# A fourth K pair by seven products in the strips of both up projections

## The chip, the cores and the metric

The kernel runs on one core of one Trainium2 chip. The metric is the device time of one execution in microseconds. The kernel before takes 2373.14 us, the median of 3 runs (2372.95 to 2373.27).

## The reference, cut to what matters

```python
D_MODEL, SEQ, FFN_HIDDEN = 2048, 256, 5632

def swiglu(x, w_up, w_down):
    g, u = jnp.split(x @ w_up, 2, axis=-1)
    return (jax.nn.silu(g) * u) @ w_down

h = h + 0.5 * rms_norm(swiglu(rms_norm(h, ffn1_pre), ffn1_up, ffn1_down), ffn1_post)
h = h + rms_norm(hybrid_mixer(rms_norm(h, mix_pre), ...), mix_post)
h = h + 0.5 * rms_norm(swiglu(rms_norm(h, ffn2_pre), ffn2_up, ffn2_down), ffn2_post)
```

All is float32 with 256 tokens. `x @ w_up` is 256 x 2048 by 2048 x 11264; its left half is the gate, its right half the upper part. Each of the two feed-forward blocks has such an up projection, and the change is in these two.

## The kernel before

A float32 product is made of three fp32r matmuls: high part by high part, low part by high part, high part by low part (the helper `three`, and the same in `products`). So each weight block that TensorE (PE) takes must first be split: SyncE loads 256 rows x 512 columns (a "group", 128 partitions x 1024 elements, 512 KB) into one of four slots of `w_raw`; ScalarE (ACT) rounds it to `w_hi` (`round_group`, L1260); VectorE (DVE) subtracts to get `w_lo` (`rest_group`, L1641). Both work four groups ahead of TensorE: at loop position n they treat group n+4, and the rounding waits until TensorE has used group n in the same slot. SyncE loads into a slot of `w_raw` again as soon as DVE has made `w_lo` of it, and, where sums are made of it, once these are made too (`up_loads`).

An up projection is cut into 11 strips of 512 gate columns and the 512 upper columns that go with them. The first strip is a stage of its own (`first0`, `first1`), computed plainly. The other ten (`NST`) are a loop, the stages `up0` and `up1`. A strip has 16 groups, of which eight are for the gate and eight for the upper part; K (2048) is eight K groups ("pairs", since each has two tiles of 128 rows). Plain, a pair takes one gate group and one upper group, each 2 row tiles x 2 token tiles x 3 matmuls, so 24 matmuls of 512 columns for both.

Three pairs (`QUADS`) are computed otherwise, with seven block products in place of eight, in the manner of Strassen and Winograd: over the 2 x 2 blocks (two row tiles; gate and upper) sums of weight blocks are multiplied by sums of token blocks, 21 matmuls in all. The token sums `s_hi`, `s_lo` are made once, in the stage `first`. The weight sums are made anew for each pair in each strip:

- `sum13` (DVE, L1829) makes two of four sums at once, 1024 elements, and needs both groups of the pair landed; it stands ahead of the `rest_group` of the pair's gate group;
- `sum24` (DVE, L1837 and L1839) makes the third and the fourth, 512 elements each, behind that `rest_group`;
- ACT rounds the four sums in two instructions of 1024 elements (L1458), at the positions in `T_AT`, and DVE subtracts in two instructions of 1024 elements (L2024), behind the `rest_group` of the same positions. For a pair whose gate group is ng these positions are ng-3 and ng-2;
- of the pair's upper group only half need be split (`w_cols`), 512 elements in place of 1024.

Two buffers hold the sums (`T_SLOT`), and `sum13` waits on `t_used` for the one it writes. TensorE computes a pair at the position of its upper group (`seven_products`, L870 to L872), in this order: two products with split weights of the gate group, one of the upper group, then two products for which it waits for the first of the two splits of sums (`t_split`), one for which it waits for the second, and one more. Four PSUM banks collect products of all pairs of a strip; DVE combines them in four instructions at n = 13, two at n = 14, and four, with two block transposes, after the last group (L2030 to L2055, L1978).

In the last strip DVE and ACT also split the first two parts of the hidden activations (`hidden_hi`, `hidden_lo`, L1680) at n = 12 to 14, which the first matmul of the stage `down` needs. All engines take their instructions in order; the order is written out by hand.

Of the kernel before, what the change touches and what calls it, by code (L numbers as in the profile page):

```python
# [23 lines left out]
P = 128  # L24
D = 2048
SEQ = 256
MT = SEQ // P
# [23 lines left out]
WARM_UP = 2  # L51


QUADS = ((5, 6, 5), (9, 10, 6), (12, 13, 7))
PLAIN_GATE = ((0, 0), (1, 1), (2, 2), (3, 3), (4, 4))
PLAIN_UP = ((7, 0), (8, 1), (11, 2), (14, 3), (15, 4))
NQUAD = len(QUADS)
NST = NUP - 1
S_TILES = 2 * NQUAD
# [92 lines left out]
def hybrid_trunk(nc, t, out):  # L152
    f32, f32r = mybir.dt.float32, mybir.dt.float32r
# [16 lines left out]
    with ctx:  # L170
# [3 lines left out]
        def sb(name, shape, dt, at=None):  # L174
            size = 4
            for n in shape[1:]:
                size *= n
            if at is None:
                at = place["at"]
                place["at"] += -(-size // 32) * 32  # L180
            return nc.alloc_sbuf_tensor_at(name, shape, dt, offset=at)

        h = sb("h", [P, MT, D], f32)
        x_at = place["at"]
# [43 lines left out]
        r_end = r_hi + 4 * KF * SEQ  # L228
# [10 lines left out]
        s_x = r_hi + 32 * 2 * STRIP  # L239
        s_raw = sb("s_raw", [P, 4, NQUAD, P], f32, at=s_x)  # L240
        s_lo = sb("s_lo", [P, 4, NQUAD, P], f32r, at=s_x)
        s_hi = sb("s_hi", [P, 4, NQUAD, P], f32r, at=s_x + 16 * NQUAD * P)
        assert s_x + 32 * NQUAD * P <= r_end
        h_scaled = sb("h_scaled", [P, S_TILES * P], f32, at=r_hi)
        a_tile0 = sb("a_tile0", [P, S_TILES, P], f32, at=r_hi + 4 * S_TILES * P)
        a_tile1 = sb("a_tile1", [P, S_TILES, P], f32, at=r_hi + 8 * S_TILES * P)
# [118 lines left out]
        t_used = sem("t_used")  # L365
# [7 lines left out]
        h_parked = sem("h_parked")  # L373
# [106 lines left out]
        def quad(f, i, j):  # L480

            return (NQUAD * NST + NDQ) * f + NQUAD * i + j
# [8 lines left out]

        QUAD_GATE = {ng: j for j, (ng, nu, k) in enumerate(QUADS)}
        QUAD_UP = {nu: j for j, (ng, nu, k) in enumerate(QUADS)}
        DQ_A = [{ng: j for j, (ng, nu, k) in enumerate(quads)} for quads in DOWN_QUADS]
        DQ_B = [{nu: j for j, (ng, nu, k) in enumerate(quads)} for quads in DOWN_QUADS]
        T_SLOT = (1, 0, 1)

        COMBINED = ("u4", "hid")

        def wait_combined(eng, f, i, what):  # L500

            eng.wait_ge(combined, len(COMBINED) * (NST * f + i) + COMBINED.index(what) + 1)

        def w_cols(sec, i, n):

# [3 lines left out]
        def t_pair(a, j, pair):  # L509

            return a[:, T_SLOT[j], 2 * pair:2 * pair + 2, :]

        T_AT = {ng - 3 + pair: (j, pair) for j, (ng, nu, k) in enumerate(QUADS) for pair in range(2)}

# [10 lines left out]
        def wait_quad_used(eng, f, i, j):  # L525

            eng.wait_ge(t_used, quad(f, i, j) + 3)
# [16 lines left out]
        SQUARES, at = {}, 0  # L544
# [23 lines left out]
        def _(sp):  # L568
# [14 lines left out]
            def up_loads(f):  # L583
                for n in range(2 * GD):
                    load(f"first{f}", 0, n, up[f][n % GD][:, :, (n // GD) * FFN:(n // GD) * FFN + STRIP])
                    if f == 0 and n in (0, 1, 3, 4):
# [3 lines left out]
                        else:  # L590
                            load_x((n + 2) // 2)
                source = {n: (k, 0) for n, k in PLAIN_GATE}
                source.update({n: (k, FFN) for n, k in PLAIN_UP})
                for ng, nu, k in QUADS:
                    source[ng], source[nu] = (k, 0), (k, FFN)
# [167 lines left out]
        def _(pe):  # L763
# [110 lines left out]
            def scaled_transposes(f):  # L874

                pe.wait_ge(h_scaled_ready, f + 1)
                for b, tiles in ((2, range(0, 2)), (3, range(2, S_TILES))):
                    claim(f"s{f}", b)
                    for x in tiles:
                        last = transpose(bank[b][:, x % 4 * P:(x % 4 + 1) * P], h_scaled[:, x * P:(x + 1) * P])  # L880
                    last.then_inc(filled[b], 1)

            def seven_products(f, i, j):

                sec = f"up{f}"
                ng, nu, k = QUADS[j]
                first, last = j == 0, j == NQUAD - 1
# [12 lines left out]
                def tt(y):  # L900
                    return t_hi[:, T_SLOT[j], y, :], t_lo[:, T_SLOT[j], y, :]

# [69 lines left out]
            def swiglu(f):  # L972
# [15 lines left out]
                with pe.Fori(0, NST) as i:  # L988
                    sec = f"up{f}"
                    gate_of, up_of = dict(PLAIN_GATE), dict(PLAIN_UP)  # L990
                    for n in range(2 * GD):
# [256 lines left out]
        def _(act):  # L1248
# [179 lines left out]
            def swiglu(f):  # L1428
                sec = f"first{f}"
                for n in range(2 * GD):  # L1430
                    round_group(sec, 0, n)
                    if f == 0 and n in (0, 2):
                        x_hi(n // 2 + 2)
                    if n == (3 if f == 0 else 2):
                        if f == 0:
                            for c in range(CH):
                                act.wait_ge(x_landed[c], 16)
                        input_squares(2 * f)
                    if n == GD - 1:
                        wait_strip(act, sec, 0, n)  # L1440
                        act.wait_ge(rs_ready, MEAN[f"pre{2 * f}"] + 1)
                        pair = pair_of(sec, 0)
                        for m in range(MT):
                            last = act.activation(gate_sb[:, m, :], acc[pair][m][:, :], ACT.Silu,
                                                  scale=rs_pre[:, 2 * f, m:m + 1])
                        last.then_inc(acc_read[pair], 1)
                    if n == 14:
                        act.wait_ge(s_summed, f + 1)
                        act.activation(s_hi[:, :, :, :].rearrange("p a b n -> p (a b n)"),
                                       s_raw[:, :, :, :].rearrange("p a b n -> p (a b n)"), ACT.Copy).then_inc(s_rounded, 1)  # L1450
                sec = f"up{f}"
                with act.Fori(0, NST) as i:
                    for n in range(2 * GD):
                        round_group(sec, i, n)
                        if n in T_AT:
                            j, pair = T_AT[n]
                            act.wait_ge(t_summed, 3 * quad(f, i, j) + 2 * pair + 1)
                            act.activation(t_pair(t_hi, j, pair), t_pair(t_raw, j, pair), ACT.Copy).then_inc(t_rounded, 1)  # L1458
                        if n == 12:
                            wait_filled(act, f"p{f}", 0, i)  # L1460
                            act.activation(p1_sb[:, :], bank[0][:, :], ACT.Copy).then_inc(read[0], 1)
                        if n == 15:
                            wait_strip_read(act, sec, i, 0)
                            for m in range(MT):
                                last = act.activation(gate_sb[:, m, :], gate_sb[:, m, :], ACT.Silu,
                                                      scale=rs_pre[:, 2 * f, m:m + 1])
                            last.then_inc(silu_done, 1)
                        if n in (12, 13):
                            with act.If(i > NST - 2):
                                if n == 12:  # L1470
                                    wait_quad_used(act, f, NST - 1, 1)
                                hidden_hi(f, n - 12)
                if f == 0:
                    act.wait_ge(consts_landed, 16 * NCONST)
                wait_quad_used(act, f, NST - 1, NQUAD - 1)
                for i in range(CH // 2):
                    down_strips(f, i)
# [150 lines left out]
        def _(dve):  # L1628
# [162 lines left out]
            def scaled_turned(f):  # L1791

                gain = pre_gain[:, 2 * f, :]
                for b, tiles in ((2, range(0, 2)), (3, range(2, S_TILES))):
                    wait_filled(dve, f"s{f}", b)
                    for x in tiles:
                        last = dve.tensor_scalar(a_tile1[:, x, :], bank[b][:, x % 4 * P:(x % 4 + 1) * P],
                                                 gain[:, S_K0 + x:S_K0 + x + 1], None, ALU.mult)
                    if b == 2:
                        last.then_inc(read[b], 1)  # L1800
                last.then_inc(read[3], 1)
# [20 lines left out]
            def sum13(f, i, j):  # L1822

                sec, (ng, nu, k) = f"up{f}", QUADS[j]
                b = quad_blocks(j)
                dve.wait_ge(t_used, quad(f, i, j) + (2 if j == 0 else 1))
                dve.wait_ge(w_landed[ng % SLOTS], group_landed(sec, i, ng))
                dve.wait_ge(w_landed[nu % SLOTS], group_landed(sec, i, nu))
                dve.tensor_tensor(t_pair(t_raw, j, 0), b[:, 0::3, :], b[:, 2:3, :].broadcast_to([P, 2, STRIP]),  # L1829
                                  ALU.add).then_inc(t_summed, 1)  # L1830

            def sum24(f, i, j):

                b = quad_blocks(j)
                t = t_raw[:, T_SLOT[j], :, :]
                dve.wait_ge(t_summed, 3 * quad(f, i, j) + 1)
# [484 lines left out]
```

## Time and profile before

| | |
|---|---|
| median of 3 runs | 2373.14 us |
| the profiled execution | 2372.41 us, its span 2370.6 us |
| TensorE busy, share of the span | 2356.8 us, 99% |
| VectorE busy | 1750.5 us, 74% |
| ScalarE busy | 1243.2 us, 52% |
| GpSimd busy | 205.9 us, 9% |
| DMA | 477.44 MB, mean 201 GB/s |
| TensorE clock granted, mean | 0.999 of full speed |

Busy time is the union of an engine's instructions. The profile's duration of a matmul, 389 ns, is from its start to its modelled end, and matmuls overlap: what counts is the distance from start to start. On DVE too an instruction starts somewhat before the end of the one ahead is shown, so costs on it are also read from start to start. The lines of the trace give the start in us, the duration in us, engine, line of the kernel, operation and tiles; in square brackets stands how long the engine had been idle and what released it.

### The profile page before, as it was taken

To read this page: it belongs to the slowest core of one execution; us is meant where nothing else is said; L and a number is where in the kernel's file an instruction comes from. 1 tells how busy PE (TensorE), PEld (TensorE's weight loads), DVE (VectorE), ACT (ScalarE), POOL (GpSimd) and SP (SyncE) were. 2 spreads that over 40 slices of the span, in tenths; PEclk is the share of its full clock that TensorE was granted. 3 is DMA by queue.
4 is the path that set the end of the run, shared out by engine and by line. 5 is a ranking of instruction groups with operands and counts; after the bars stand their busy time and mean duration, and the time that the engine had idled before them with its cause. 6 is when DMAs were issued, how large, how long until landed. Compare 5 with 4: busy or idle time off the path is not lost. (4 is left out here: it accounts for less than half of the span.)

```text
span 2370.6 us, 33710 instructions
## 1 busy us (share of the span) xinstructions
PE 2356.8 (99%) x10613; PEld 1945.0 (82%) x10613; DVE 1750.5 (74%) x2057; ACT 1243.2 (52%) x1490; POOL 205.9 (9%) x398
## 2 busy tenths in 40 slices
PE   9999999999999999999999999999999999999998
PEld 7888888888888888888888888888888888888887
DVE  6999999978876555655545545555799999997886
ACT  6555555555545454444544444444655555555553
POOL 1212112110000000000000000000021211211000
PEclk9999999999999999999999999999999999999999
DMA  7766666665675555565656566655666666666665
GB/s 236 220 212 203 216 219 222 212 221 191 209 240 172 163 175 178 159 188 157 204 187 196 190 198 193 189 185 194 207 213 227 206 218 207 221 212 214 204 204 195
DMA packets 266605, 477.44 MB, mean 201 GB/s; under 512 B 21152, under 2 KB 54608, under 8 KB 265392
## 3 DMA queue, kind: packets, MB, share of 16 engines
q1 hardware_dynamic: 252752, 453.04, 59.6%
q0 software_dynamic: 13616, 23.53, 3.0%
q8 instruction: 35, 0.57, 0.1%
q14 instruction: 26, 0.21, 0.0%
q10 hardware_dynamic: 176, 0.07, 0.0%
HBM read 460.84 MB, written 4.19 MB: 196 GB/s over the span
## 5 line engine op out<-in xcount | busy, mean ns | idle before, releaser
L1260 ACT ACTIVATE w_hi<-w_raw 128x1024 fp32r<-128x1024 f32 (+1 forms) x848 | 863.6, 1021 | 985.9 <-PE acc L781 732.1
L1641 DVE TENSOR_TENSOR w_lo<-w_raw,w_hi 128x1024 fp32r<-128x1024 f32 (+1 forms) x848 | 991.8, 1172 | 507.5 <-ACT w_hi L1260 503.0
L779 PE MATMUL acc<-w_hi,xT_hi 128*128 128x512 f32 x1552 | 609.2, 393 | 1.0 <-DVE w_lo L1641 1.0
L781 PE MATMUL acc<-w_hi,xT_lo 128*128 128x512 f32 x1552 | 604.4, 389 | 0.0
L780 PE MATMUL acc<-w_lo,xT_hi 128*128 128x512 f32 x1552 | 604.1, 389 | 0.0
L779 PEld LDWEIGHTS acc<-w_hi,xT_hi 128*128 128x128 f32 x1552 | 291.4, 188 | 63.0 <-issue 2.5
L781 PEld LDWEIGHTS acc<-w_hi,xT_lo 128*128 128x128 f32 x1552 | 291.3, 188 | 61.1
L780 PEld LDWEIGHTS acc<-w_lo,xT_hi 128*128 128x128 f32 x1552 | 291.5, 188 | 59.3
L696 POOL DMA_DIRECT2D act_raw<-blocks x352 | 174.9, 497 | 736.4 <-DVE blocks L1978 647.5
L779 PE MATMUL acc<-w_hi,act_hi 128*128 128x512 f32 x560 | 218.2, 390 | 0.1
L780 PE MATMUL acc<-w_lo,act_hi 128*128 128x512 f32 x560 | 217.9, 389 | 0.0
L781 PE MATMUL acc<-w_hi,act_lo 128*128 128x512 f32 x560 | 217.9, 389 | 0.0
L870 PE MATMUL acc<-w_hi,xT_hi 128*128 128x512 f32 x460 | 178.9, 389 | 0.0
L871 PE MATMUL acc<-w_lo,xT_hi 128*128 128x512 f32 x460 | 178.9, 389 | 0.0
L872 PE MATMUL acc<-w_hi,xT_lo 128*128 128x512 f32 x460 | 178.9, 389 | 0.0
L2024 DVE TENSOR_TENSOR t_lo<-t_raw,t_hi 128x1024 fp32r<-128x1024 f32 x120 | 146.2, 1218 | 0.0
L1458 ACT ACTIVATE t_hi<-t_raw 128x1024 fp32r<-128x1024 f32 x120 | 126.8, 1057 | 31.1 <-DVE t_raw L1829 22.1
L779 PEld LDWEIGHTS acc<-w_hi,act_hi 128*128 128x128 f32 x560 | 105.2, 188 | 22.6 <-DVE act_lo L1680 0.9
L781 PEld LDWEIGHTS acc<-w_hi,act_lo 128*128 128x128 f32 x560 | 105.1, 188 | 21.8
L780 PEld LDWEIGHTS acc<-w_lo,act_hi 128*128 128x128 f32 x560 | 105.1, 188 | 21.8
L871 PEld LDWEIGHTS acc<-w_lo,xT_hi 128*128 128x128 f32 x460 | 86.3, 188 | 18.0
L870 PEld LDWEIGHTS acc<-w_hi,xT_hi 128*128 128x128 f32 x460 | 86.3, 188 | 17.9
(269 smaller groups left out, 2601.4 us busy)
## 6 DMA issues: line engine op xcount, KB each, us to landing
w_raw<-in_ffn_up_dram SPq DMA_DIRECT2D x352, 512.0 KB, 4.2
w_raw<-in_ffn_down_dram SPq DMA_DIRECT2D x176, 512.0 KB, 4.2
w_raw<-in_w_gate_dram SPq DMA_DIRECT2D x96, 512.0 KB, 3.8
w_raw<-in_w_in_dram SPq DMA_DIRECT2D x72, 512.0 KB, 3.6
w_raw<-in_w_in_dram SPq DMA_DIRECT2D x128, 256.0 KB, 2.9
w_raw<-in_w_ret_out_dram SPq DMA_DIRECT2D x32, 512.0 KB, 3.7
w_raw<-in_w_out_dram SPq DMA_DIRECT2D x32, 512.0 KB, 4.2
act_raw<-blocks POOLq DMA_DIRECT2D x352, 32.0 KB, 3.8
```

Source lines behind the costliest of these rows:

```text
L696: pool.dma_start(act_raw[to * SQ:(to + 1) * SQ, ds(p, 1), q, :, :, :].rearrange("p a m k i -> p (a m) k i"), blocks[q * SQ:(q + 1) * SQ, t ...
L779: pe.matmul(pair[m][:, :], xh, wh, start=(first and kk == 0), stop=False)
L780: pe.matmul(pair[m][:, :], xh, wl, start=False, stop=False)
L781: mm = pe.matmul(pair[m][:, :], xl, wh, start=False, stop=(last and kk == KG - 1))
L870: pe.matmul(dst, xh, wh, start=start, stop=False)
L871: pe.matmul(dst, xh, wl, start=False, stop=False)
L872: return pe.matmul(dst, xl, wh, start=False, stop=stop)
L1260: act.activation(w_hi[:, s, cols], w_raw[:, s, cols], ACT.Copy).then_inc(w_rounded, 1)
L1458: act.activation(t_pair(t_hi, j, pair), t_pair(t_raw, j, pair), ACT.Copy).then_inc(t_rounded, 1)
L1641: dve.tensor_tensor(w_lo[:, s, cols], w_raw[:, s, cols], w_hi[:, s, cols].bitcast(f32), ALU.subtract).then_inc(w_split, 1)
L2024: dve.tensor_tensor(t_pair(t_lo, j, pair), t_pair(t_raw, j, pair), t_pair(t_hi, j, pair).bitcast(f32), ALU.subtract).then_inc(t_split, 1)
```

## The change

QUADS gets a fourth member. K pair 4 (gate group 4, upper group 5) is added, and pair 5 moves from groups 5 and 6 to groups 6 and 7; pairs 6 and 7 stay at 9, 10 and 12, 13. Four gate groups and four upper groups stay plain. The pairs take the two buffers of sums in turn. The arrays of token sums grow from six tiles to eight (`S_TILES`), so two more transposes and longer DVE and ACT instructions in `first0` and `first1`. The array `s_hi` moves to the place of the residual h; for the second block the instruction that writes it waits until h has been stored to memory (`h_parked`).

```diff
-QUADS = ((5, 6, 5), (9, 10, 6), (12, 13, 7))
-PLAIN_GATE = ((0, 0), (1, 1), (2, 2), (3, 3), (4, 4))
-PLAIN_UP = ((7, 0), (8, 1), (11, 2), (14, 3), (15, 4))
+QUADS = ((4, 5, 4), (6, 7, 5), (9, 10, 6), (12, 13, 7))
+PLAIN_GATE = ((0, 0), (1, 1), (2, 2), (3, 3))
+PLAIN_UP = ((8, 0), (11, 1), (14, 2), (15, 3))
...
-        s_hi = sb("s_hi", [P, 4, NQUAD, P], f32r, at=s_x + 16 * NQUAD * P)
-        assert s_x + 32 * NQUAD * P <= r_end
+        s_hi = sb("s_hi", [P, 4, NQUAD, P], f32r, at=x_at - 4 * MT * D)
+        assert s_x + 16 * NQUAD * P <= r_end
...
-        T_SLOT = (1, 0, 1)
+        T_SLOT = (0, 1, 0, 1)
...
+        PARKED = 16 * MT * 1
...
-                for b, tiles in ((2, range(0, 2)), (3, range(2, S_TILES))):
+                for b, tiles in ((2, range(0, 4)), (3, range(4, S_TILES))):
...
                     if n == 14:
                         act.wait_ge(s_summed, f + 1)
+                        if f == 1:
+                            act.wait_ge(h_parked, PARKED)
                         act.activation(s_hi[:, :, :, :].rearrange("p a b n -> p (a b n)"),
...
                                 if n == 12:
-                                    wait_quad_used(act, f, NST - 1, 1)
+                                    wait_quad_used(act, f, NST - 1, 2)
...
-                dve.wait_ge(t_used, quad(f, i, j) + (2 if j == 0 else 1))
+                dve.wait_ge(t_used, quad(f, i, j) + 1)
```

The line with the tiles changes the same way on DVE (`scaled_turned`).

## Rows read from the trace of the kernel before

**Rows 1.** The page: shares of the span, DVE in slices, ACT's rounding of weights.

```profile
PE 2356.8 (99%) x10613; PEld 1945.0 (82%) x10613; DVE 1750.5 (74%) x2057; ACT 1243.2 (52%) x1490; POOL 205.9 (9%) x398
...
DVE  6999999978876555655545545555799999997886
...
L1260 ACT ACTIVATE w_hi<-w_raw 128x1024 fp32r<-128x1024 f32 (+1 forms) x848 | 863.6, 1021 | 985.9 <-PE acc L781 732.1
```

**Rows 2.** Windows: the stages up0 and up1; header row names the columns.

```profile
core 0: us, PE busy (x) PEld busy (x) DVE busy (x) ACT busy (x) POOL busy (x), PEclk, DMA share, GB/s
57.40:472.20 414.80, 414.80 (x1831) 343.24 (x1829) 388.07 (x429) 234.27 (x253) 79.47 (x160) 1.00 0.67 215
...
1713.70:2128.50 414.80, 414.80 (x1831) 343.28 (x1829) 387.99 (x430) 234.32 (x253) 79.52 (x160) 1.00 0.67 215
```

**Rows 3.** Timeline of TensorE: transposes; first up0 matmul; last; first of down0.

```profile
11.57 1.03 PE L800 MATMUL bank<-ident,h 128*128 128x128 f32 x8
...
57.35 0.39 PE L779 MATMUL acc<-w_hi,xT_hi 128*128 128x512 f32 x1
...
471.93 0.39 PE L872 MATMUL acc<-w_hi,xT_lo 128*128 128x512 f32 x1
472.39 0.50 PE L779 MATMUL acc<-w_hi,act_hi 128*128 128x512 f32 x1
```

**Rows 4.** Timeline of DVE: end of one strip and most of the next.

```profile
142.75 0.68 DVE L2048 TENSOR_TENSOR hid_sb<-acc,u_sb 128x512 f32<-128x512 f32 x1
...
146.87 1.18 DVE L1641 TENSOR_TENSOR w_lo<-w_raw,w_hi 128x1024 fp32r<-128x1024 f32 x1
147.97 1.21 DVE L1829 TENSOR_TENSOR t_raw<-w_raw 128x1024 f32<-128x1024 f32 x1
149.10 1.22 DVE L1641 TENSOR_TENSOR w_lo<-w_raw,w_hi 128x1024 fp32r<-128x1024 f32 x1
150.24 0.68 DVE L1837 TENSOR_TENSOR t_raw<-t_raw,w_raw 128x512 f32<-128x512 f32 x1
150.96 0.69 DVE L1839 TENSOR_TENSOR t_raw<-t_raw,w_raw 128x512 f32<-128x512 f32 x1
151.56 0.68 DVE L1641 TENSOR_TENSOR w_lo<-w_raw,w_hi 128x512 fp32r<-128x512 f32 x1
152.17 1.22 DVE L2024 TENSOR_TENSOR t_lo<-t_raw,t_hi 128x1024 fp32r<-128x1024 f32 x1
...
158.00 1.23 DVE L1829 TENSOR_TENSOR t_raw<-w_raw 128x1024 f32<-128x1024 f32 x1 [1.21 <-DMA w_raw<-in_ffn_up_dram]
...
165.99 1.23 DVE L1829 TENSOR_TENSOR t_raw<-w_raw 128x1024 f32<-128x1024 f32 x1 [0.29 <-DMA w_raw<-in_ffn_up_dram]
...
175.19 1.23 DVE L1641 TENSOR_TENSOR w_lo<-w_raw,w_hi 128x1024 fp32r<-128x1024 f32 x1 [0.36 <-ACT w_hi L1260]
176.62 1.23 DVE L1641 TENSOR_TENSOR w_lo<-w_raw,w_hi 128x1024 fp32r<-128x1024 f32 x1 [0.20 <-ACT w_hi L1260]
177.76 0.68 DVE L2030 TENSOR_TENSOR u_sb<-p_sb,bank 128x512 f32<-128x512 f32 x1
...
180.37 1.23 DVE L1641 TENSOR_TENSOR w_lo<-w_raw,w_hi 128x1024 fp32r<-128x1024 f32 x1
```

**Rows 5.** DMA issues: source, queue, count, KB each, median us to landing.

```profile
w_raw<-in_ffn_up_dram SPq DMA_DIRECT2D x352, 512.0 KB, 4.2
...
out_dram<-h POOLq DMA_DIRECT2D x2, 1024.0 KB, 4.1
```

**Rows 6.** Timeline of DVE: the passage from first0 into up0.

```profile
60.26 1.75 DVE L2000 TENSOR_TENSOR s_lo<-s_raw,s_hi 128x1536 fp32r<-128x1536 f32 x1
...
64.59 1.18 DVE L1641 TENSOR_TENSOR w_lo<-w_raw,w_hi 128x1024 fp32r<-128x1024 f32 x1
```

**Rows 7.** Timeline of DVE: the last strip of up0.

```profile
462.23 1.22 DVE L2024 TENSOR_TENSOR t_lo<-t_raw,t_hi 128x1024 fp32r<-128x1024 f32 x1
...
471.05 1.29 DVE L1680 TENSOR_TENSOR act_lo<-act_raw,act_hi 128x512 fp32r<-128x512 f32 x2
```

**Rows 8.** Timeline of GpSimd: the second store of h.

```profile
1672.48 0.53 POOL L752 DMA_DIRECT2D out_dram<-h  x1 [3.69 <-DVE h L1713]
```

More of the change, by code:

```diff
@@ L1793, in scaled_turned @@
                 gain = pre_gain[:, 2 * f, :]
-                for b, tiles in ((2, range(0, 2)), (3, range(2, S_TILES))):
+                for b, tiles in ((2, range(0, 4)), (3, range(4, S_TILES))):
                     wait_filled(dve, f"s{f}", b)
```

## Prediction

> **What bounds the kernel now.** I read the shares of the span first: TensorE is busy 99% of it, DVE 74% [rows 1]. That alone says that whatever takes matmuls away is won. The slices say that it is not so simple: DVE stands at nine tenths or more in slices 2 to 8 and 30 to 36, which are the stages up0 and up1 [rows 1]. The windows of the two stages give the sizes: in 414.80 us TensorE is busy all of it and DVE 388.07 us, 94% [rows 2]. So in the stages that the change touches, the second engine is 27 us short of the first, over ten strips. Then I read TensorE's timeline for its pace and DVE's timeline for one strip, row by row.
>
> TensorE: the first matmul of up0 starts at 57.35, the last at 471.93 [rows 3]. A strip has 10 plain groups of 12 and three pairs of 21, 183 matmuls; ten strips make 1830, and 414.58 us over 1829 steps is 0.2267 us from start to start, 41.48 us for a strip. A product (three matmuls) is 0.68 us. TensorE's clock is granted in full, 1.00 [rows 2], the 2.4 GHz level.
>
> DVE, from start to start [rows 4]: a full split of weights 1.14 (149.10 to 150.24), a half split 0.60 (151.56 to 152.17), `sum13` 1.13 (147.97 to 149.10), `sum24` 1.32 (150.24 to 151.56), a split of two sums 1.14 (as the weight split of the same length, 1.22 us shown for both). The blocks: four instructions at n = 13 take 2.61 (177.76 to 180.37), two at n = 14 take 1.20 (twice 0.60), the six at the end of the strip 4.12 (142.75 to 146.87). A strip before: 13 full splits 14.82, 3 half 1.80, three pairs at 1.13 + 1.32 + 2.28 = 4.73 make 14.19, blocks 7.93: together 38.74 us. The rest of the 41.48, 2.74 us, is waiting.
>
> **The change, part by part.**
>
> TensorE: one pair of 24 matmuls becomes one of 21. 3 x 0.2267 = 0.68 us less for a strip, 40.80 us for 180 matmuls; over 20 strips 13.6 us.
>
> DVE: one more pair, +4.73 us, and one full split that becomes half, -0.54: +4.19 us for each strip, 42.93 us of its own work. That is more than the 40.80 that TensorE needs, and also more than the 41.48 that a strip takes today. So the bound changes engine. The durations are of one kind of instruction and of fixed length in the rows, so I see nothing that would stretch or shrink them.
>
> Which of DVE's waits stay? The waits for ACT's rounding that itself waited for TensorE go away, since TensorE now runs behind. Those for data stay. The two groups loaded into the slots of pair (12, 13) are fetched only once its sums are made; the load takes 4.2 us to land [rows 5], then ACT rounds 1.0 us [rows 1]. DVE meets them at 175.19 and 176.62 with 0.36 and 0.20 us idle [rows 4]; since an idle also loses the usual overlap of 0.08, these are 0.72 us. That stretch of the order is the same in the new strip, so I keep 0.7. The `sum13` of pair (12, 13) waits 0.29 for its group [rows 4] in this strip; I keep 0.2. The wait of 1.21 us at 158.00 for group 10 [rows 4] I let go: today group 10 is fetched when the half split of group 6 is done (152.24) and is wanted after four full instructions; in the new order it is fetched after the sums of pair (6, 7), and DVE has 0.60 and four times 1.14, 5.2 us, until it wants it, against the 4.2 of the load. The bounds of this wait are 0 and 0.6 (today's 158.00 - 152.24 = 5.8 us less 5.2); I take 0, because today's load is queued 0.6 us behind another one and this one isn't. A strip then takes 42.93 + 0.7 + 0.2 = 43.8 to 43.9; I use 43.87, 2.39 more than today. TensorE waits 43.87 - 40.80 = 3.07 us in each.
>
> Where it waits: the pairs (4, 5) and (6, 7) lie side by side behind the longest block of DVE. From the last split of sums of pair (12, 13) to the second split of pair (4, 5) DVE has three full splits 3.42, the waits 0.7, blocks of 2.61 + 1.14 + 1.20 + 1.14 + 4.12, and then `sum13`, full, `sum24`, half, split, `sum13` of the next pair, full, `sum24`, split: 10.05. That is 24.4 us. TensorE has 31 products there, 21.1 us. In the remaining part of the strip DVE needs 19.4 us and TensorE, with 29 products, 19.7, so it doesn't wait there and DVE is 0.3 us ahead at the end of it. The whole wait should therefore stand at one place, the third product with sums (L870, bank<-t_hi,s_hi) of pair (4, 5), released by DVE L2024. Does DVE wait for TensorE in turn? `sum13` of pair (9, 10) needs the buffer of pair (4, 5), which is free 1.6 us after the wait ends, and DVE reaches it after 4.0 us. The fourth plain group ahead, whose rounding needs the end of the strip on TensorE plus 1.0 for ACT, is ready about 0.5 us before DVE wants it. Both hold, the second narrowly.
>
> The first strip: DVE's split of token sums is 512 elements longer. 512 elements are the difference of 1.22 and 0.68 us [rows 4], 0.54, so `s_lo` takes 2.29 in place of 1.75, and `sum13` of pair (4, 5) starts at 64.59 + 0.54 = 65.1 [rows 6]. The second split of sums starts 8.9 later and ends at 75.3. TensorE reaches the product that needs it after 48 + 15 matmuls, 57.35 + 14.28 = 71.6. It waits 3.6 and saves 0.68: +2.9 us.
>
> The end of the stage: in the last strip today the last split of sums ends at 462.23 + 1.22 = 463.45 [rows 7], and TensorE starts the product that needs it ten products before the stage's end (471.93 + 0.23 = 472.16 [rows 3]), at 472.16 - 6.80 = 465.36, so DVE is 1.9 us ahead. The first matmul of down0 starts at 472.39 instead of 472.16 [rows 3], just behind the split of hidden activations (471.05 + 1.29) [rows 7]. With a lead of 0.3 this split comes 1.6 us later: +1.6 us.
>
> A stage: 2.9 + 9 x 2.39 + 1.6 = 26.0 us. Two stages: 52.0 us, since up1 shows the same busy times [rows 2].
>
> The stages first0 and first1: two more transposes in each, eight take 1.03 us [rows 3], so 0.13 each, 0.5 us in all. The longer ACT and DVE instructions there lie beside TensorE's work except the one counted above. ACT's added work in up is two roundings of sums less half a rounding of weights, some 1.7 us for a strip, on an engine that is busy 234.27 of 414.80 us [rows 2]; nothing. The wait for the stored h: the second store is issued at 1672.48 [rows 8] and takes 4.1 us to land [rows 5], while the stage up1 begins only at 1713.70 [rows 2] and the waiting instruction stands a group and a half of DVE's lead ahead of that, over 30 us after the landing; nothing. If it did wait, the four rounded groups ahead, 10.9 us of TensorE, would cover it. SyncE gets two more waits for sums in each strip, with the loads behind them; they delay only loads counted above.
>
> The sum is 52.5 us against the profiled execution's 2372.4: 2424.9. The median of the runs is 0.7 above that execution, so 2425.6; I give 2425.
>
> **The rivals.**
>
> *TensorE stays the bound.* Then the time falls by 13.6 - 0.5 us to 2360. This needs DVE to do a strip in 40.8 us; from 41.48 on it would be no slower than today. Against it: 42.93 us of instructions of a fixed length [rows 4], with no wait counted. For it only that 27 us of DVE idle [rows 2] cover ten times 2.7 us, not the ten times 4.2 us that are added. I give it 5%, most of it for a mistake in my count of instructions.
>
> *The loads come late too.* DVE frees the slots later than today and two pairs side by side want four groups within 12 us. If group 10 is late by 0.6 and pair (12, 13) or (6, 7) by as much as today's 1.21 us [rows 4] in part, a strip grows by 0.6 to 1.2 us: 2437 to 2449. For it: such a wait stands in the rows today. Against: DMA moves the same bytes in more time, its share is 0.67 [rows 2], and the margins above are positive. 15%.
>
> *The clock falls in the waits.* TensorE would stand still for 3 us in each strip, and in the rows it never does so in these stages; at 1.00 throughout [rows 2], they can't say what it does. If as long a time as the wait ran at the 1.2 GHz level, TensorE would lose 1.5 us, of which DVE's lead and its margin hide some 0.8. The rest, 0.7 to 1.0 for each strip, gives about 2442. The Trainium skill (TensorE: Matmul & The Clock Gate, section HAM oscillation) warns of this, that a kernel whose TensorE waits for data in every round of its loop can be throttled anew in every round; no row here shows it, and by it the time would be that of this rival. 8%.
>
> **How the numbers follow.** The forecast, DVE the bound with the waits as counted, has 72%, and a range of its own of 2410 (no waits left, 42.93 for a strip: 18 x 0.94 = 17 less, and not all of that) to 2432 (a third of a microsecond more for a strip). The others have 5, 15 and 8%. For 8 in 10 I take the forecast's range and the lower half of the late loads: 2408 to 2440. About 0.2% is what a measurement of this kernel can tell from no change, 4.7 us: slower 0.94, faster 0.04, the same 0.02, the last two shares of the first rival.
>
> **What would show it.** Right: in the strips' windows DVE is busy about 98% and TensorE below 94%; a strip is 43.9 us long from L2048 to L2048; among TensorE's waits one for t_lo L2024 with about 60 us in 20 times, each near 3 us, and none of size elsewhere; DVE's waits on w_hi fall from 1.3 us for a strip to under 0.7. Wrong: waits of DVE for DMA above 0.5 us for a strip (late loads), a granted clock under 1.00 in the stage, or matmuls 0.2267 us apart through whole strips (TensorE the bound). The prediction fails as a whole if DVE's instructions in a strip are not 12 full splits, 4 half ones, 20 for the sums and 12 in the blocks.

## The result and the profile after

The changed kernel takes 2440.09 us, the median of 4 runs (2438.72 to 2442.03), against 2373.20 for the kernel before, a ratio of 1.0282 (95% interval 1.0268 to 1.0296): 66.9 us slower. Slower was forecast, with 52 us and a range that ended at 2440.0; the time lies just outside it, where two of the rivals were put: the falling clock (2442) and the late loads (2437 to 2449).

The profiled execution takes 2442.03 us, its span is 2440.2. The page gives for busy time and slices (compare [rows 1]):

```profile
PE 2373.6 (97%) x10557; PEld 1947.9 (80%) x10557; DVE 1835.2 (75%) x2161; ACT 1271.7 (52%) x1530; POOL 204.8 (8%) x398
...
DVE  6999999978777655656545554556799999997886
```

The next block is the list of waits of TensorE, longest in total first (what waited, for whom, us in total, times, longest). Before, TensorE waited nowhere in the up stages.

```profile
PE bank L872 <- DVE t_lo L2028: 51.3, 22, 3.1
PE acc L1038 <- DVE gate_sb L2071: 2.0, 1, 2.0
```

The wait stands where the forecast put it: at the third product with sums of the first pair (line 870 is 872 now, 2024 is 2028). It comes once in each of the 20 strips, at 2.3 to 3.1 us, and twice more for 0.2. Now four strips of up0, from L2052 (before L2048) to L2052, as windows, and in the last line eight strips of up1; the columns are those of [rows 2].

```profile
107.50:152.46 44.96, 42.68 (x181) 34.90 (x181) 43.04 (x50) 24.82 (x28) 7.94 (x16) 0.96 0.63 199
152.46:196.67 44.21, 41.93 (x184) 34.11 (x184) 42.77 (x49) 24.86 (x29) 7.95 (x16) 1.00 0.63 198
...
285.97:332.07 46.10, 43.13 (x178) 35.11 (x178) 43.04 (x50) 24.19 (x27) 7.94 (x16) 0.93 0.62 196
...
422.04:465.88 43.84, 41.56 (x183) 34.07 (x183) 42.76 (x49) 24.74 (x28) 7.95 (x16) 1.00 0.63 200
...
1800.35:2155.66 355.31, 335.68 (x1444) 274.78 (x1444) 343.16 (x386) 197.51 (x218) 63.53 (x128) 0.98 0.63 200
```

Two things are to be seen. DVE is busy 42.8 to 43.0 us in every strip, as counted (42.93). And the length of a strip goes with the granted clock, the column of 1.00, 0.96 or 0.93: in up0 those at full clock have 43.8 to 44.5 us, the fastest 43.84 against the forecast's 43.87, and those with less clock 44.8 to 46.1. Over eight strips of up0 the mean is 44.80. In up1 strips of 44.95 at 0.96 and of 43.8 to 43.9 at 1.00 take turns, and the mean is 44.41. What the clock does is seen in TensorE's timeline around one wait:

```profile
296.90 0.39 PE L874 MATMUL bank<-t_hi,s_lo 128*128 128x512 f32 x1
300.25 0.79 PE L872 MATMUL bank<-t_hi,s_hi 128*128 128x512 f32 x1 [2.97 <-DVE t_lo L2028]
300.84 0.63 PE L873 MATMUL bank<-t_lo,s_hi 128*128 128x512 f32 x1
301.27 0.63 PE L874 MATMUL bank<-t_hi,s_lo 128*128 128x512 f32 x1
```

Behind the wait the matmuls are 0.43 us apart (300.84 to 301.27), not 0.23: the 1.2 GHz level. It lasts for 13 matmuls here, 2.6 us lost. In up0 7 of the 10 waits are followed by some 7 to 13 such slow starts, 3 by none; in up1 it is 6 of 10.

### The profile page after: what moved, and what is told of

It reads as the page before. It is cut to its first block and busy times, and to the rows that moved or that the text cites. A ratio compares the mean times of both kernels' runs of the same rounds, so it can differ in the third digit from the quotient of the medians.

```text
span 2440.2 us, 34075 instructions
## 1 busy us (share of the span) xinstructions
PE 2373.6 (97%) x10557; PEld 1947.9 (80%) x10557; DVE 1835.2 (75%) x2161; ACT 1271.7 (52%) x1530; POOL 204.8 (8%) x398
## 5 line engine op out<-in xcount | busy, mean ns | idle before, releaser
L781 PE MATMUL acc<-w_hi,xT_hi 128*128 128x512 f32 x1472 | 578.2, 393 | 1.2 <-DVE w_lo L1645 1.0
L783 PE MATMUL acc<-w_hi,xT_lo 128*128 128x512 f32 x1472 | 573.2, 389 | 0.0
L782 PE MATMUL acc<-w_lo,xT_hi 128*128 128x512 f32 x1472 | 573.0, 389 | 0.0
L781 PEld LDWEIGHTS acc<-w_hi,xT_hi 128*128 128x128 f32 x1472 | 276.4, 188 | 60.6 <-issue 3.2
L783 PEld LDWEIGHTS acc<-w_hi,xT_lo 128*128 128x128 f32 x1472 | 276.3, 188 | 57.9
L782 PEld LDWEIGHTS acc<-w_lo,xT_hi 128*128 128x128 f32 x1472 | 276.5, 188 | 55.9
L1462 ACT ACTIVATE t_hi<-t_raw 128x1024 fp32r<-128x1024 f32 x160 | 169.5, 1060 | 107.0 <-DVE t_raw L1833 80.2
L2028 DVE TENSOR_TENSOR t_lo<-t_raw,t_hi 128x1024 fp32r<-128x1024 f32 x160 | 194.8, 1217 | 0.0
L872 PE MATMUL acc<-w_hi,xT_hi 128*128 128x512 f32 x400 | 156.6, 392 | 0.0
L873 PE MATMUL acc<-w_lo,xT_hi 128*128 128x512 f32 x400 | 156.3, 391 | 0.0
L874 PE MATMUL acc<-w_hi,xT_lo 128*128 128x512 f32 x400 | 155.9, 390 | 0.0
L872 PE MATMUL bank<-t_hi,s_hi 128*128 128x512 f32 x240 | 98.7, 411 | 51.3 <-DVE t_lo L2028 51.3
L872 PEld LDWEIGHTS bank<-t_hi,s_hi 128*128 128x128 f32 x240 | 45.9, 191 | 69.5 <-DVE t_lo L2028 61.0
```

The costliest lines, as they stand in the source:

```text
L781: pe.matmul(pair[m][:, :], xh, wh, start=(first and kk == 0), stop=False)
L782: pe.matmul(pair[m][:, :], xh, wl, start=False, stop=False)
L783: mm = pe.matmul(pair[m][:, :], xl, wh, start=False, stop=(last and kk == KG - 1))
L872: pe.matmul(dst, xh, wh, start=start, stop=False)
L873: pe.matmul(dst, xh, wl, start=False, stop=False)
L874: return pe.matmul(dst, xl, wh, start=False, stop=stop)
```

## The experiments

Five theories were put to the chip. A: DVE's work for a strip sets 43.9 us, and the rest of the loss is the clock that falls in TensorE's waits. B: all of the loss is DVE's work, of which I counted too little. C: a busier TensorE holds up DVE. D: the place of the two first pairs side by side makes TensorE wait, whatever DVE's total. E, formed after the first four runs: a chain that starts anew at the end of each strip on TensorE and runs over ACT and DVE. "Half of a weight group" below means that the low parts of the other half stay as they were. Each ratio is against the kernel before on the same chip.

**Ten filling matmuls in the wait.**

```diff
                 p5 = three(bank[1][:, :], *s(0), *tt(0), first, last)
+                if first:
+                    for _ in range(10):
+                        pe.matmul(bank[2][:, :], s(2)[0], tt(1)[0], start=True, stop=True)
                 pe.wait_ge(t_split, 2 * quad(f, i, j) + 2)
```

> The changed kernel with ten more matmuls of 512 columns (2.27 us) on TensorE in every strip of both up loops, ahead of its wait for the second split of sums of the first pair; what they write to the bank is overwritten. They fill most of the 2.3 to 3.1 us for which TensorE stands still there. Theory A (DVE sets 43.9 us for a strip, and the rest of the loss is a clock that falls in the waits): the slow matmuls (0.43 us apart) go, the granted clock is 1.00 in the stages, a strip is 43.9 us, the time about 2425. Theory B (all of the loss is DVE's own work and waits, of which I counted too little): no gain, 2438 to 2442. Theory C (a busier TensorE delays DVE through the slots): 2445 or more.

2427.85 us, ratio 1.0230 (1.0213 to 1.0247). TensorE is given 20 x 2.27 us more work and the kernel is 12 us faster. The window over eight strips, of the changed kernel and of this one:

```profile
107.50:465.00 357.50, 337.79 (x1439) 275.52 (x1439) 342.53 (x385) 196.68 (x217) 63.53 (x128) 0.97 0.63 199
```
```profile
107.50:465.00 357.50, 352.94 (x1546) 288.96 (x1545) 347.78 (x392) 199.71 (x220) 65.04 (x131) 1.00 0.64 201
```

The clock is 1.00 and no slow starts are left in the strips, whose mean is 43.99 us (43.74 in up1). B and C fall and A holds as far as this goes: with the clock up a strip takes what was counted for DVE, and 12 us are the clock's.

**Five filling matmuls.** The same edit with `range(5)`.

> The changed kernel with five filling matmuls in place of ten (1.13 us), so TensorE stands still for 1.2 to 2.0 us in each strip. If it is the length of the standstill that lets the clock fall, and 1.2 to 2.0 us is short enough, 2425 to 2429 as with ten; if any standstill does it, 2432 to 2440.

2428.12 us, ratio 1.0231 (1.0214 to 1.0248), as with ten, and a mean strip of 43.75 us. TensorE still waits:

```profile
PE bank L872 <- DVE t_lo L2031: 31.4, 22, 1.9
```

31.4 us in 22 waits, the longest 1.9. One of the 20 in the strips, the first in up1 with 1.95 us, is followed by eight slow starts, the others by none:

```profile
1761.88 0.50 PE L872 MATMUL bank<-t_hi,s_hi 128*128 128x512 f32 x1 [1.95 <-DVE t_lo L2031]
...
1763.06 0.63 PE L873 MATMUL acc<-t_lo,xT_hi 128*128 128x512 f32 x1
1763.48 0.63 PE L874 MATMUL acc<-t_hi,xT_lo 128*128 128x512 f32 x1
```

At the end of up0, where TensorE waits 1.8 us for the hidden activations, some eight slow ones follow too. So waits of 1.1 to 1.95 us were followed by the lower clock once in 20, those of 2.3 to 3.1 us in the changed kernel 13 times in 20. No length parts the two cases: in the kernel with eight half groups, below, two of up0's nine waits of 1.76 us were followed by eight or nine slow starts and none of up1's nine, and in the one with the closing block moved a wait of 3.08 us, the first of up1, was followed by none.

**Half of eight weight groups split on DVE.**

```diff
                 s, cols = n % SLOTS, w_cols(sec, i, n + SLOTS)
+                if sec in ("up0", "up1") and n + SLOTS in (8, 11, 14, 15, 16, 17, 18, 19):
+                    cols = slice(STRIP, KG * STRIP)
```

> The changed kernel, but DVE splits only half of each of eight plain weight groups in a strip (512 elements in place of 1024, 4.3 us less for DVE; the low parts of the other half are left as they were, so the result is inexact). TensorE, ACT, loads and order are unchanged. Theory A and B (DVE's work is the bound): DVE needs 38.6 us and some 0.9 of waits, under TensorE's 40.8; the time is the 2360 us that the 13.6 us of saved matmuls promise. Theory D (the place of the two pairs side by side makes TensorE wait, whatever DVE's total): the wait for the sums stays, above 2400.

2413.63 us, ratio 1.0169 (1.0152 to 1.0186). I expected 2360. DVE's total is down to 38.6 us, below TensorE's 40.8, and a strip with the clock up still takes 42.87. Neither A nor B explains that. The rows of one strip, from the timelines of TensorE, ACT and DVE:

```profile
192.91 0.39 PE L781 MATMUL acc<-w_hi,xT_hi 128*128 128x512 f32 x1
...
193.11 1.06 ACT L1262 ACTIVATE w_hi<-w_raw 128x1024 fp32r<-128x1024 f32 x1 [1.66 <-PE acc L874]
...
194.21 0.69 DVE L1647 TENSOR_TENSOR w_lo<-w_raw,w_hi 128x512 fp32r<-128x512 f32 x1 [0.83 <-ACT w_hi L1262]
194.82 0.68 DVE L2054 TENSOR_TENSOR hid_sb<-acc,u_sb 128x512 f32<-128x512 f32 x1
...
198.94 1.18 DVE L1835 TENSOR_TENSOR t_raw<-w_raw 128x1024 f32<-128x1024 f32 x1
...
207.84 1.22 DVE L2030 TENSOR_TENSOR t_lo<-t_raw,t_hi 128x1024 fp32r<-128x1024 f32 x1
...
209.11 0.50 PE L872 MATMUL bank<-t_hi,s_hi 128*128 128x512 f32 x1 [1.76 <-DVE t_lo L2030]
```

Read it as a chain. TensorE ends a strip and starts the next at 192.91; only then may ACT round the weights four groups ahead (193.11); DVE, idle for 0.83 us, splits them (194.21), closes the strip (4.12 us, to 198.94) and makes sums and splits for two pairs (8.90 us, to the start of the first pair's second split at 207.84); 0.05 us after the end of that split, shown as 1.22 us long, TensorE goes on, 16.20 us after the strip began. On its own it would have been there after 14.3 (63 steps of 0.2267). DVE idles before the chain starts, so its total is no help: this is a second bound, 1.9 us for each strip. That is theory E, and half of D.

**Half of four groups.** The same edit with (8, 11, 14, 15), none of which lies in that chain.

> As the one before with four plain groups split by half (2.16 us less for DVE; low parts of the other half left as they were). DVE needs 40.8 us and 0.9 of waits, 41.7 for a strip against 40.8 of TensorE, which waits 0.9 us at one place. Theory A: such a short wait leaves the clock up, so a strip is 41.7 us, 2380 us in all (2376 to 2386). Theory B (I count too little for DVE by 0.9 us a strip, whatever the clock): 42.6 us a strip, about 2397.

2437.82 us, ratio 1.0273 (1.0256 to 1.0290). It removes 2.16 us of DVE for each strip and gains 2 us in all (I expected 2376 to 2386, or 2397). The strips are 43.4 and 43.7 us where the clock stayed up and 45.0 where it fell. By E the chain here is 16.20 + 0.54 = 16.74 (a full split in place of the half one), a wait of 2.4 and a strip of 43.2. Measured from the first matmul of a strip to the end of its wait are 16.7 to 16.8 us in 16 of the 18 strips that follow another in the loop. Both of my numbers were missed for want of E.

**The kernel before with 3.42 us more for DVE in a strip.**

```diff
+                if sec in ("up0", "up1") and n + SLOTS in (4, 8, 12):
+                    dve.tensor_tensor(spare[:, :], w_raw[:, s, :], w_hi[:, s, :].bitcast(f32), ALU.subtract)
                 dve.tensor_tensor(w_lo[:, s, cols], w_raw[:, s, cols], w_hi[:, s, cols].bitcast(f32), ALU.subtract).then_inc(w_split, 1)
```

> The kernel before with three more DVE instructions of 1024 elements in every strip (a weight split made once more into unused memory, 3.42 us); no other work is changed. DVE then needs 42.16 us and 0.9 of waits, 43.1 for a strip against TensorE's 41.48. Theory A without a fall of the clock 2373 + 20 x 1.6 = 2405, with falls up to 2420, and the waits lie at the last or first pair's sums. If DVE's load is not what sets the strip, the time stays at 2373.

2408.57 us, ratio 1.0147 (1.0130 to 1.0164): 35.7 us slower, 32 expected. The strips of up0 are 42.8 to 43.4 us, 43.17 in the mean (43.00 in up1), where 43.1 was worked out. So the kernel before had just the room that its 2.74 us of DVE waits showed, and no token sum or new place of a pair is needed to lose time.

**Sums on GpSimd.** The third and fourth sums of pairs (9, 10) and (12, 13), then of all four pairs, made by GpSimd instead of DVE.

```diff
+            def pool_sum24(f, i, j):
+                pool.wait_ge(t_summed, 3 * quad(f, i, j) + 1)
+                pool.tensor_tensor(t_[:, 2, :], t_[:, 0, :], b[:, 3, :], ALU.add).then_inc(p_summed, 1)
+                wait_pool_sums(pool, f, i, j, 1)
+                pool.tensor_tensor(t_[:, 3, :], t_[:, 2, :], b[:, 1, :], ALU.add).then_inc(p_summed, 1)
```

> The changed kernel with the third and fourth sum of the two late pairs, (9, 10) and (12, 13), made by GpSimd in place of DVE (2.64 us less for DVE in a strip, nothing left out). Theory A (DVE's total alone): DVE needs 40.3 us and 0.9 of waits, so a strip is 41.2 us and the time about 2370. Theory E (a chain through the strip's end: TensorE ends the strip, ACT rounds 1.06, DVE splits 1.14, closes the strip 4.12 and makes the sums and splits of the first two pairs 10.05, before TensorE can take a product that it reaches 14.28 us after the strip's end): this chain is untouched, a strip stays at 43.3 us and more where the clock falls, 2415 to 2440. GpSimd's two sums of 512 elements should take 1 to 2 us each; if they slow DVE's instructions, the time is above 2440.

> The same for all four pairs (5.28 us less for DVE in a strip); GpSimd issues the transfers of the hidden blocks in two halves, between its sums. Theory E: the chain is shorter by 2.64 us, its last split ends 14.0 us after the strip's end against TensorE's 14.28, and DVE's total of 37.65 us leaves room, so TensorE is the bound at 40.8 us a strip or just above: 2360 to 2370, faster than the kernel before. Theory A gives the same here. If GpSimd needs over 2 us for a sum, its sums are late and the wait at the first pair stays: 2400 or more.

2511.59 us (1.0588, 1.0571 to 1.0606) and 2539.75 us (1.0697, 1.0679 to 1.0714), far slower, where 2415 to 2440 and 2360 to 2370 were expected; the expectations named GpSimd sums that slow DVE or take over 2 us as what would make them miss. GpSimd takes mostly 2.2 us for the third sum and 1.6 for the fourth, at most 2.8, where DVE takes 0.68, and DVE itself slows down meanwhile. Two rows of one timeline each, of the run with all four pairs:

```profile
218.45 1.62 POOL L709 TENSOR_TENSOR t_raw<-t_raw,w_raw 128x512 f32<-128x512 f32 x1
```
```profile
218.84 2.31 DVE L2060 TENSOR_TENSOR t_lo<-t_raw,t_hi 128x1024 fp32r<-128x1024 f32 x1
```

The same split takes 1.22 us in the kernel before; its mean over 200 us of this run is 1.76, that of the half weight splits 1.78 in place of 0.68. DVE is busy 44.0 us for a strip of up0 with two pairs on GpSimd and 46.4 with four, against 42.9, so it was not relieved. With two pairs it also waits more, 3.6 us a strip against 1.5 in the changed kernel; what is added are waits for loads and for GpSimd's sums. So these runs tell nothing about E. The runs show only that DVE slows beside GpSimd, not by what path. The Trainium skill (GPSIMD Engine Reference, section Specifications) states that the two share their interfaces to SBUF and that DVE instructions with two inputs in SBUF contend for them; the splits are of that kind, and the 2.31 us agree.

**The closing block later.** Two multiplications and two transposes of the closing block (2.8 us) moved into the next strip, behind the splits of the second pair; first in the kernel with eight half groups, then in the changed kernel.

```diff
+                        if n == 5:
+                            with dve.If(i > 0):
+                                close_strip(before(i, NST))
...
-                    wait_strip_read(dve, sec, i, 1)
-                    for m in range(MT):
-                        last = dve.scalar_tensor_tensor(hid_sb[:, m, :], hid_sb[:, m, :], rs_pre[:, 2 * f, m:m + 1],
...
-                    turn_blocks()
```

> The run with eight half splits (DVE 4.3 us less, low parts of the other halves left as they were), and in it the last part of the strip's closing block on DVE (two multiplications and two transposes, 2.8 us, L2059 and L1982) made in the next strip, behind the splits of sums of the second pair. DVE does the same work. Theory E (a chain from the end of the strip on TensorE through ACT and DVE to the sums): the second split of the first pair ends 13.3 us after the strip's end in place of 16.1, before TensorE gets there (14.3), so that wait goes; the later pairs' sums come 0.2 to 1.0 us late. A strip is 41.0 to 41.8 us in place of 42.87, the time 2364 to 2380. If the wait has another cause, it stays at 2413.

2392.78 us, ratio 1.0088 (1.0071 to 1.0105), 21 us less than without the move, and a mean strip of 41.85 (41.67 in up1) in place of 42.87. DVE does the same work, only in another order, and from the second strip on the wait at the first pair goes. The strip is at the upper edge of where E put it, 41.0 to 41.8; the time is 13 us above the expected 2364 to 2380. That range left out the ends of the loops: from TensorE's starts, the first strips of up0 and up1 are 6.1 and 4.6 us longer than before, the last ones 1.8 each. What still holds the strip above 40.8 no run shows. `sum13` of the fourth pair waits for its weights in each strip, some 0.9 us,

```profile
215.69 1.23 DVE L1835 TENSOR_TENSOR t_raw<-w_raw 128x1024 f32<-128x1024 f32 x1 [0.91 <-DMA w_raw<-in_ffn_up_dram]
```

but without the move it did so too, some 0.7 us. TensorE loses its 1.0 us in pieces of 0.35 us and less, at the sums of the later pairs and at the strip's start.

> The changed kernel with the same 2.8 us of the closing block moved behind the second pair's sums; all work done. DVE's total stays 42.9 us and 0.9 of waits. Theory E and DVE's total together: the chain now binds at the third pair, at 42.9 us, so DVE's total sets 43.9 us and a slow stretch of TensorE up to 1 us is absorbed; 2425 to 2437, against 2440. If the place of the closing block does not matter, 2440.

2429.83 us, ratio 1.0238 (1.0221 to 1.0256). As expected: with DVE's total unchanged, strips are 43.96 us in the mean (43.83 in up1), and what is gained, 10 us, is the clock, which stays at 1.00 from the second strip on, where TensorE's wait is cut into pieces of 0.6 us and less. The first strip of each stage, which the move leaves as it was, still has its wait of 3.1 us and seven or eight slow starts.

**The first pair's second split earlier.** The most direct test of where the wait comes from, with all work done.

```diff
-        T_AT = {ng - 3 + pair: (j, pair) for j, (ng, nu, k) in enumerate(QUADS) for pair in range(2)}
+        T_AT = {}
+        for j, (ng, nu, k) in enumerate(QUADS):
+            for pair in range(2):
+                T_AT.setdefault(ng - 3 + (pair if j else 0), []).append((j, pair))
```

> The changed kernel with one move, all work done: the second rounding and split of sums of the first pair (4, 5) stand behind the first ones, ahead of the second pair's sum13, weight split and sum24 (3.6 us of DVE). Theory E: TensorE gets those sums 3.6 us sooner and does not stand still there for 2 to 3 us any more; DVE's total still sets a strip, 43.7 to 43.9 us, the waits are spread over the later pairs and the clock stays up: 2425 to 2430. If the standstill is only moved as one piece and the clock falls as before, 2437 to 2440.

2433.36 us, ratio 1.0254 (1.0237 to 1.0272). The long standstill is gone, the longest wait for splits of sums is 0.6 us, and the clock is up:

```profile
PE bank L875 <- DVE t_lo L2029: 17.8, 48, 0.6
PE bank L875 <- DVE w_lo L1647: 6.1, 21, 0.6
```

The time is 3 us above what I expected: strips have 44.11 us (43.99 in up1) in place of 43.8. TensorE now waits some five times a strip. Why DVE's strip is 0.2 to 0.3 us longer than with five filling matmuls I have not settled.

**The same and half of twelve groups.**

> The same move, and DVE splits only half of each of twelve weight groups in a strip (6.5 us less for DVE, low parts of the other halves left as they were). Both bounds, DVE's total (36.4 us) and the chain from the strip's end over DVE to each pair's sums, are then below TensorE's 40.8 us at every pair. The saved matmuls should show: 40.8 to 41.0 us a strip, 2360 to 2366. If something else than DVE (loads, ACT, the slots of weights) holds the strip, it stays above 2373.

2367.80 us, ratio 0.9979 (0.9969 to 0.9988), against 2372.88 for the kernel before. The window over eight strips:

```profile
107.50:465.00 357.50, 357.50 (x1579) 296.13 (x1578) 319.44 (x418) 214.89 (x240) 71.69 (x144) 1.00 0.67 218
```

TensorE is busy all of it, and a strip has 40.80 us (40.65 to 40.82), 180 times 0.2267. This run leaves work out and is no kernel to keep, but it shows where the expected gain is: all 0.68 us of a strip are there once DVE's total and the chain are both below TensorE. In the strips the loads and ACT are not in the way here. The whole is 5.1 us faster, not 13.6, and 1.8 above the expected 2360 to 2366: by TensorE's starts the first strip of each stage takes 44.0 and 43.7 us, against 41.48 in the kernel before, and the last one 41.9 and 42.4 against 41.7 and 41.6. No run of the changed kernel with all work done was faster than the kernel before; the best is 2428.

## Why the forecast was right in kind and short in size

*TensorE's and DVE's work for a strip.* Right. 0.2267 us from start to start, and 42.93 us of DVE counted against 42.8 to 43.0 measured. The change of the bound, on which the sign hung, is shown from both sides: by the kernel before with DVE work added and by the changed one with DVE work taken away.

*The waits of DVE.* Right in the sum (43.87 a strip; 43.84 in the best strip of the changed kernel, 43.75 in the mean with the clock held up). The wait of 1.21 us for group 10 did go: over eight strips of up0 DVE waits 1.6 us for loads, 8.0 before. At 0.2 us a strip that also rules out the rival with late loads, whose range held the measured time. The waits on ACT's rounding were to fall from 1.3 us a strip to under 0.7; in the changed kernel they are 1.3 (1.1 in up1), with the clock held up 0.6.

*The place of the standstill.* Right, as the waits show, with 2.3 to 3.1 us instead of 3.07. That it stood in one piece was given no price; the runs that filled it or cut it up gained 7 to 12 us.

*The clock.* This is the step that failed. The forecast took the clock as 1.00 and gave its fall 8%, with a price of 0.7 to 1.0 us a strip and about 2442 us. Measured are 44.80 - 43.87 = 0.93 us a strip in up0, 0.54 in up1, and 12 us in all by the filling matmuls (2440.1 to 2427.9). The price was about right, the chance too low. The Trainium skill (TensorE: Matmul & The Clock Gate, section HAM oscillation) was weighed there, that a TensorE that waits for data in every round of a loop can be throttled anew in every round; here it was in 13 of 20 rounds. The rows of before have no wait of TensorE in these stages, so no row stood behind the 8%.

*The margin of half a microsecond.* I checked that DVE needn't wait for TensorE and found the chain over the strip's end free by 0.5 us. I did not draw the conclusion that, with the first pair at 14.3 us, the chain alone makes 43.2 us a strip. By the count the total, 43.87, still binds, so the sum did not change. But in the changed kernel the two bounds take turns. One strip of each kind, its first matmul and the end of its wait:

```profile
105.07 0.39 PE L781 MATMUL acc<-w_hi,xT_hi 128*128 128x512 f32 x1
121.79 0.80 PE L872 MATMUL bank<-t_hi,s_hi 128*128 128x512 f32 x1 [2.28 <-DVE t_lo L2028]
...
193.49 0.44 PE L781 MATMUL acc<-w_hi,xT_hi 128*128 128x512 f32 x1
210.97 0.79 PE L872 MATMUL bank<-t_hi,s_hi 128*128 128x512 f32 x1 [2.97 <-DVE t_lo L2028]
```

In 11 of the 18 strips that follow another in the loop the wait is 2.28 us and ends 16.73 us after the strip began, as the chain has it; in the other seven it is 2.7 to 3.0 and ends after 17.1 to 17.5, by DVE's total. So a fall of the clock is handed on to the next strip: TensorE ends the strip later, DVE starts the chain later, and the next wait ends later by as much. It is also why taking 2.16 us off DVE bought nothing. All seven of the longer waits were followed by slow starts, and four of the 11 shorter ones.

*The first strip.* Forecast +2.9 us. By TensorE's starts it takes 41.48 us in the kernel before and 46.04 in up0 with five filling matmuls, the clock up: +4.6. In the changed kernel 1.6 us of slow starts come on top. The words "The longer ACT and DVE instructions there lie beside TensorE's work" were wrong. ACT and DVE of the changed kernel at that place, from the timelines:

```profile
57.71 1.92 ACT L1453 ACTIVATE s_hi<-s_raw 128x2048 fp32r<-128x2048 f32 x1 [1.71 <-DVE s_raw L1819]
...
60.61 1.23 DVE L1645 TENSOR_TENSOR w_lo<-w_raw,w_hi 128x1024 fp32r<-128x1024 f32 x1 [1.79 <-ACT w_hi L1262]
61.75 2.29 DVE L2004 TENSOR_TENSOR s_lo<-s_raw,s_hi 128x2048 fp32r<-128x2048 f32 x1
...
66.62 1.18 DVE L1833 TENSOR_TENSOR t_raw<-w_raw 128x1024 f32<-128x1024 f32 x1
```

DVE's longer token sums hold up ACT's rounding of them, that holds up the rounding of weights behind it, and DVE waits 1.79 us for these. `s_lo` has the 2.29 us that were worked out, but starts at 61.75 in place of 60.26 [rows 6], and `sum13` at 66.62 instead of 65.1. The term was short by 1.7 us for each of two stages.

*The end of the stage.* Forecast +1.6 us. In the changed kernel TensorE waits only 0.2 us there, at the end of up0, after a last strip with slow starts; with five filling matmuls it waits 1.8, and 1.3 at the end of up1. There, with five, the wait of up0 is followed by some eight slow starts (1.6 us), which belong to the clock again.

*The sum.* With the clock held up the changed kernel stands at 2428, 3 us above the forecast, about what the first strips were short by (2 x 1.7). The other 12 are the clock.

*What was costed at nothing.* The wait for the stored h, the loads behind two more waits of SyncE and ACT's two more roundings left no wait in the rows that would speak against it.

## What to carry to other kernels

Before matmuls are saved with sums on another engine, add up that engine's instructions from start to start for one round; DVE's 94% was 2.7 us of room for an edit of 4.2. Then follow, from the point at which the round starts anew, what the helping engine must do until each product that waits for it: that is a bound of its own, and idle time that the helper has ahead of that chain doesn't shorten it. Where a forecast ends with the matrix engine standing still in one piece in each round, price the clock as likely, not as a rival; here splitting the standstill or filling it gave back 7 to 12 us, though not enough to pay for the change.

## What was not expected of the hardware

TensorE with 1.13 us of useless matmuls in each of 20 waits made the kernel 12 us faster (2440.1 to 2428.1), and ten did no better than five. Waits of equal length differ: of two of 2.28 us in the changed kernel's up0, one was followed by seven slow starts and the next by none. GpSimd's additions of 512 float32 elements take 1.6 to 2.2 us mostly, and beside them a DVE subtraction of 1024 elements took up to 2.31 us in place of 1.22.
